# A hybrid attention and mLSTM block: three loads at the start of the kernel given to other queues, and the first block of x loaded in two halves

## The chip, the cores and the metric

The kernel runs on one core of one Trainium2 chip. The metric is the device time of one execution in microseconds. Before the change it was timed three times: median 314.51 us, from 314.25 to 314.80 us. One more execution was recorded by the hardware profiler; all rows below come from that one.

## The reference

`x` has 512 tokens of 1024 features. The block is one layer:

```
h    = rms_norm(x, pre_norm_g)
proj = h @ w_in                      # 1024 x (9*512 + 8) columns
aq, ak, av, az, mq, mk, mv, mo, mz, mi, mf = split_columns(proj)
ya = moba_attention(rope(aq), rope(ak), av)          # 8 heads of 64
ya = rms_norm(ya, attn_out_g) * silu(az)
hm = mlstm_chunkwise(silu(conv(mq)), silu(conv(mk)), mv, mi, mf)   # 4 heads of 128
ym = sigmoid(mo) * normalised(hm) * mlstm_out_g * silu(mz)
y  = concat(ya, ym) @ w_out
out = x + rms_norm(y, post_norm_g)
```

All in fp32. For this change only the start matters: `x` is scaled column by column with `pre_norm_g` and multiplied with the first 512 columns of `w_in` that are wanted, those of `mv`. The rms factor of each token is applied to the products afterwards.

## The kernel before, in words

Every fp32 operand of a product is split into a high part (fp32r) and a low part (the rest), and a product is three matmuls: high by high, low by high, high by low. The weights come in blocks of 128 x 512 (256 KB), called slots, numbered in the order of a table `SLOTS`. A slot lies first in one of 4 raw buffers (`w_raw`), its high part is made by ScalarE (`cut`, line 797) and its low part by VectorE (line 1072). Slot 0 is the exception: its high part is made by VectorE (line 1099).

`x` (`x_sb`, which the profile names by its arena, `farena`) is loaded in six column chunks: four of 128 columns (256 KB) and two of 256 columns (512 KB). A chunk of 128 columns is 512 rows of 512 bytes. TensorE turns each 128 x 128 block of x with `ident` into a PSUM bank (line 1542 for the first 128 columns, line 1549 for later ones). ScalarE writes the high part of the turned x, scaled with the gains of the norm (line 803 in two halves of 256 tokens for the first block, line 809 for later ones), and VectorE writes the low part (lines 1095 and 1088). The gains come as 8 rows of 128 in the tile `prow` (4 KB), which TensorE turns too (line 1537), and VectorE copies them from PSUM to `pcol` (line 1083).

All engines run their own list of instructions in order. What sets the order at the start:

- SyncE's queue (SP) issues, in this order, chunk 0 of x, weight slot 0, chunk 1 of x, slot 1, chunk 2, slot 2 and so on. From slot 4 on each issue waits until the low part of the slot four places earlier is made.
- ScalarE issues `prow` as its first instruction (line 826), then loads its activation table, and then waits for the first turned half of x.
- GpSimd clears `ident` (line 613), clears `prow2` (line 614), makes `ident` the identity (line 616), and then waits for the high part of slot 0 before its next work (lines 619 and on). Its own loads (lines 637 to 645: six small ones into `prow2`, one into `rope_sb`) come after that.
- VectorE waits for the turned gains, copies them, waits for slot 0, makes its high part (line 1099), then the two low halves of x, then the low part of slot 0.
- TensorE runs six matmuls on constants (`keep_busy`, line 1531), waits for `ident` and for `prow`, turns `prow` (line 1537), waits for all of chunk 0 of x, turns its four blocks of tokens (line 1542, two signals, one for each half of 256 tokens), runs two more constant matmuls of 256 columns, and then starts the products of slot 0 (line 1569).

The lines of TensorE's start:

```python
            keep_busy(6)
            pe.wait_ge(ident_done, 1)
            pe.wait_ge(par_in, 16)
            pe.transpose(bank[6][:, 0:R_AG], prow[:], ident[0:R_AG, 0:R_AG]).then_inc(par_ps, 1)
            ...
            turn_x_half(0)
            turn_x_half(1)
            keep_busy(2, AW // 2)
            for k in range(NK - 1):
                mv_slot(k)
```

In a product of slot 0 to 3 (`mv_slot`) the high by high matmuls of the four token tiles come first, then (for slot 0) the low by high ones, then the blocks of the next chunk of x are turned (`turn_x(k + 1)`), and the terms with the low part of the weights come last.

Of the kernel before, what the change touches and what calls it, by code (L numbers as in the profile page):

```python
# [23 lines left out]
P = 128  # L24
# [4 lines left out]
AW = 512  # L29
# [20 lines left out]
SLOTS = [("in", "cols", k, MVC) for k in range(NK - 1)]  # L50
# [16 lines left out]
X_CHUNKS = ((0, 1), (1, 1), (2, 1), (3, 1), (4, 2), (6, 2))  # L67
# [3 lines left out]
HALF_SEQ = SEQ // 2  # L71
# [10 lines left out]
def width(n):  # L82

    return MZ_W if S_MZ <= n < S_MZ + NK else AW
# [148 lines left out]
def unit(u):  # L233

    return NT - 1 - u // AH, u % AH
# [7 lines left out]
def build(nc, x, pre_g, w_in, i_bias, f_bias, conv_w, conv_b, attn_g, mlstm_g, w_out, post_g, rope, out):  # L243
    with ExitStack() as ctx:
        def sb(name, shape, dt=F32):
            return ctx.enter_context(nc.sbuf_tensor(name, shape, dt))

        def sem(name):
            return ctx.enter_context(nc.semaphore(name))
# [4 lines left out]
        w_raw = sb("w_raw", [P, RAW, AW])  # L254
# [14 lines left out]
        prow = sb("prow", [R_AG, P])  # L269
# [34 lines left out]
        def f_part(at, *shape):  # L304
            n = int(np.prod(shape))
            v = farena[:, at:at + n]
            return v if len(shape) == 1 else v.rearrange("p (a b) -> p a b", a=shape[0]) if len(shape) == 2 \
                else v.rearrange("p (a b c) -> p a b c", a=shape[0], b=shape[1])
# [7 lines left out]
        x_sb = f_part(F_X, NT, D)  # L316
# [65 lines left out]


        x_in = [sem(f"x_in{c}") for c in range(len(X_CHUNKS))]
        par_in = sem("par_in")
        rope_in = sem("rope_in")
        post_in = sem("post_in")
        raw_in = [sem(f"raw_in{r}") for r in range(RAW)]
# [124 lines left out]
        def low_done(eng, n):  # L513

            eng.wait_ge(w_lo_done[n % 2], n // 2 + 1)
# [4 lines left out]
        def turn_tile(n):  # L520

            _, kind, i = TURNS[n]
            return 0 if kind == "ym" else 4, NT - 1 - i


        def store(sp, i):
            t = NT - 1 - i
            for c in range(2):
                cols = slice(c * AW, (c + 1) * AW)
                sp.wait_ge(out_ready, 2 * i + c + 1)  # L530
                sp.dma_start(out[0, t * P:(t + 1) * P, cols], xr[i][:, cols]).then_inc(out_done[i], 16)

        @block.sync
        def _(sp):
            x2 = x.rearrange("b s d -> (b s) d")

            def load_x(c):
                k, n = X_CHUNKS[c]
                cols = slice(k * P, (k + n) * P)
                sp.dma_start(x_sb[:, :, cols], x2[:, cols].rearrange("(t p) d -> p t d", p=P)).then_inc(x_in[c], 16)  # L540

            def rows_out(w, m):

                sp.wait_ge(kq_ready, NT * w + m + 1)
                sp.dma_start(kq_dram[w, :, ROT * m:ROT * m + ROT, :], by_dims[:, m, :]).then_inc(kq_out[w], 16)

            def rows_back(w, m):

                sp.wait_ge(kq_out[w], 16 * NT)
                if w:  # L550
                    sp.wait_ge(kt_lo, NT)
                sp.dma_start(whole[:, m, :], kq_dram[w, 2 * m:2 * m + 2].rearrange("h d s -> (h d) s"))\
                    .then_inc(kq_moved[w], 16)

            for n, (mat, kind, k, c) in enumerate(SLOTS):
                if n in X_BEFORE:
                    load_x(X_BEFORE[n])
                if n >= RAW:
                    low_done(sp, n - RAW)
                w = w_in if mat == "in" else w_out  # L560
                if kind == "cols":
                    src = w[0, k * P:(k + 1) * P, c:c + width(n)]
                    dst = w_raw[:, n % RAW, 0:width(n)]
                else:
                    src = w[0, k * P:(k + 4) * P, c:c + MD].rearrange("(k p) c -> p k c", p=P)
                    dst = w_raw[:, n % RAW, :].rearrange("p (k c) -> p k c", k=4)
                sp.dma_start(dst, src).then_inc(raw_in[n % RAW], 16)
                if n == S_QK + 6:
                    sp.wait_ge(ssx_done, NT)
                    sp.dma_start(gains[:], attn_g.to_broadcast([P, AW])).then_inc(gain_in, 16)  # L570
                for w in range(2):
                    for c in range(2):
                        if n == OUT_AT[w] + c:
                            rows_out(w, 2 * c)
                            rows_out(w, 2 * c + 1)
                        if n == BACK_AT[w] + c:
                            rows_back(w, 2 * c)
                            rows_back(w, 2 * c + 1)
                if n == S_AQ + 4:
                    sp.wait_ge(az_gained, NT)  # L580
                    sp.dma_start(gains[:], mlstm_g.to_broadcast([P, AW])).then_inc(gain_in, 16)
            sp.wait_ge(v_lo_done, NT)
            sp.dma_start(post, post_g.to_broadcast([P, D])).then_inc(post_in, 16)

            def load_residual(i):
                t = NT - 1 - i
                sp.dma_start(xr[i], x2[t * P:(t + 1) * P, :]).then_inc(xr_in[i], 16)

            sp.wait_ge(ym_gated, NT)
            load_residual(0)  # L590
            load_residual(1)
            sp.wait_ge(turn_ps, TURN_OF["ym", NT - 1] + 1)
            load_residual(2)
            load_residual(3)
            store(sp, 0)
            store(sp, 1)
            store(sp, 2)
            sp.wait_ge(out_ready, 2 * NT - 1)
            sp.dma_start(out[0, 0:P, 0:AW], xr[NT - 1][:, 0:AW]).then_inc(out_done[NT - 1], 16)
            sp.wait_ge(out_ready, 2 * NT + 1)  # L600
            sp.dma_start(out[0, 0:P, quarter[1]], xr[NT - 1][:, quarter[1]]).then_inc(out_done[NT - 1], 16)
            for i in range(NT):
                sp.wait_ge(out_done[i], 32 + 16 * (i == NT - 1))
# [3 lines left out]
        def _(g):  # L607
# [2 lines left out]

            g.memset(ident[:], 0.0).then_inc(cleared, 1)
            g.memset(prow2[:], 0.0).then_inc(par2_clear, 1)
            g.wait_ge(cleared, 1)
# [170 lines left out]
        def _(a):  # L786
# [25 lines left out]
            def x_squares(t):  # L812
                if t:
                    a.wait_ge(ssx_done, t)
                for c in range(len(X_CHUNKS)):
                    a.wait_ge(x_in[c], 16)
                a.activation(silu_az[:, 0:2, :].rearrange("p a c -> p (a c)"), x_sb[:, t, :], ACT.Square, accum_out=ssx[:, t:t + 1]).then_inc(ssx_done, 1)

# [4 lines left out]
                a.activation(mv[:, t * MH:(t + 1) * MH, 0:MD], bank[t][:].rearrange("p (h d) -> p h d", h=MH), ACT.Copy,  # L823
                             scale=rx[:, t:t + 1]).then_inc(mv_hi_done, 1)

            a.dma_start(prow[:], pre_g.rearrange("o (c p) -> (o c) p", p=P)).then_inc(par_in, 16)
            a.activation(ssx[:, 0:1], ones, ACT.Copy)
            x_hi_half(0)
            x_hi_half(1)
# [1 line left out]
            for k in range(1, NK):  # L831
                cut(k)
                x_hi(k)
                if k >= 5:
                    x_squares(k - 5)
            cut(RING)
            x_squares(NT - 1)
            for n in range(RING + 1, RING + 6):
                cut(n)
# [160 lines left out]
            for s in range(STEPS):  # L1000
# [18 lines left out]
                for kind, what in events:  # L1019
# [7 lines left out]
                    elif kind == "y_sq":  # L1027
                        i, c = what
                        n = OUT_OF[i, c]
# [5 lines left out]
                    elif kind == "y_q_sq":  # L1035
                        q = what[0]
# [476 lines left out]
        def _(pe):  # L1513
# [23 lines left out]
            pe.transpose(bank[6][:, 0:R_AG], prow[:], ident[0:R_AG, 0:R_AG]).then_inc(par_ps, 1)  # L1537

            def turn_x_half(q):
                pe.wait_ge(x_in[0], 16)  # L1540
                for t in (2 * q, 2 * q + 1):
                    mm = pe.transpose(bank[4 + q][:, t * P:(t + 1) * P], x_sb[:, t, 0:P], ident[:])  # L1542
                mm.then_inc(xt_ps, 1)
# [129 lines left out]
# [6 lines that stand above are left out]
# [42 lines left out]
            for b in range(S_QK, LAST_SLOT):  # L1721
                if b < S_MZ and (b - S_QK) % 12 < 4:
                    n = 2 * ((b - S_QK) // 12) + (b - S_QK) % 12 // 2
# [35 lines left out]
            def turn(n):  # L1759

                _, kind, i = TURNS[n]
                t = NT - 1 - i
                pe.wait_ge(ym_gated if kind == "ym" else ya_gated, i + 1)
                pe.wait_ge(masked, min(TURNS[n][0], NU))
                src = ym[:, t] if kind == "ym" else silu_az[:, t]
                for k in range(4):
                    mm = pe.transpose(bank[TURN_BANK][:, k * P:(k + 1) * P], src[:, k * P:(k + 1) * P], ident[:])  # L1767
                mm.then_inc(turn_ps, 1)
# [85 lines left out]
            for s in range(STEPS):  # L1854
# [10 lines left out]
                if 0 <= u < NU:  # L1865
                    t, h = unit(u)
# [56 lines left out]
```

## Time and profile before

| | |
|---|---|
| median of three executions | 314.51 us (314.25 to 314.80) |
| profiled execution, its time | 314.27 us |
| profiled execution, its span | 312.5 us |
| TensorE busy | 306.0 us, 98% of the span |
| VectorE, ScalarE, GpSimd busy | 73%, 53%, 29% |
| mean granted clock of TensorE | 0.995 |
| read from HBM, written | 33.68 MB, 4.28 MB |

The span is the time from the first to the last recorded instruction; the execution's own time is 1.77 us more. Times in the rows are microseconds from the start of the span. PE is TensorE's matmul side, PEld its loading of weights, DVE VectorE, ACT ScalarE, POOL GpSimd, SP SyncE; a q behind a name is the engine's sequencer, which issues DMAs.

### The profile page before, as it was taken

The page shows a single profiled execution, that of the slowest core. Times are in us where ns is not written, and L with a number is a line of the kernel's source. Part 1 is how long each engine was busy: PE and PEld are TensorE (multiplying, and loading weights), DVE is VectorE, ACT ScalarE, POOL GpSimd, SP SyncE. Part 2 cuts the span into 40 slices and gives each one's busy share as a digit, 9 for nine tenths or more (in the row PEclk, how much of TensorE's full clock was granted, in tenths as well). Part 3 has the DMA queues.
Part 4 walks back from the last instruction along what each step waited for, and adds up shares of the span by engine and source line. Part 5 has one row for each costly group of instructions (what it writes and reads, how often), then busy time and mean ns, then how long its engine had stood idle before and what let it go on. Part 6 is the DMA issues. An engine that isn't in the chain of part 4 may idle for free.

```text
span 312.5 us, 5011 instructions
## 1 busy us (share of the span) xinstructions
PE 306.0 (98%) x1607; PEld 257.4 (82%) x1607; DVE 226.8 (73%) x510; ACT 165.2 (53%) x339; POOL 91.1 (29%) x110
## 2 busy tenths in 40 slices
PE   8999999999999999999999999999999999999992
PEld 5788888888888888888888899977888888888892
DVE  2644899956999499967999457996666867856534
ACT  3467694578337324384244583574746867353301
POOL 4501005164340004000040017569612983000000
PEclk9999999999999999999999999999999999999997
DMA  7933473565423546752555432410210473310111
GB/s 208 338 77 96 105 203 100 159 196 143 151 67 97 157 144 183 215 168 72 156 184 155 130 103 67 135 69 1 81 55 2 139 222 125 141 51 0 69 68 67
DMA packets 28953, 38.28 MB, mean 123 GB/s; under 512 B 2552, under 2 KB 16236, under 8 KB 28928
## 3 DMA queue, kind: packets, MB, share of 16 engines
q1 hardware_dynamic: 27440, 34.51, 37.2%
q0 software_dynamic: 1328, 3.32, 3.0%
q8 instruction: 13, 0.21, 0.3%
q10 hardware_dynamic: 160, 0.14, 0.1%
q14 instruction: 12, 0.10, 0.1%
HBM read 33.68 MB, written 4.28 MB: 121 GB/s over the span
## 4 chain that ended last, share of the span: by engine, by line
PE 94%; issue 3%; DVE 0%; DVEq 0%; ACT 0%; POOLq 0%; POOL 0%; ACTq 0%
PE bank L1516 25%; PE bank L1518 24%; PE bank L1517 24%; PE bank L1569 4%; PE bank L1873 3%; PE bank L1817 3%; PE bank L1838 3%; PE bank L1664 2%; PE bank L1767 1%; PE bank L1531 1%; PE bank L1549 1%; PE bank L1828 1%; PE bank L1665 1%; PE bank L1850 0%; PE bank L1542 0%
## 5 line engine op out<-in xcount | busy, mean ns | idle before, releaser
L797 ACT ACTIVATE w_hi<-w_raw 128x512 fp32r<-128x512 f32 (+1 forms) x73 | 44.4, 615 | 62.9 <-PE bank L1518 50.1
L1516 PE MATMUL bank<-w_hi,xT_hi 128*128 128x512 f32 (+2 forms) x180 | 71.1, 395 | 0.0
L1518 PE MATMUL bank<-w_hi,xT_lo 128*128 128x512 f32 (+2 forms) x180 | 68.1, 379 | 0.0
L1517 PE MATMUL bank<-w_lo,xT_hi 128*128 128x512 f32 (+2 forms) x180 | 67.8, 376 | 0.0
L1516 PE MATMUL bank<-xT_hi,w_hi 128*128 128x512 f32 x136 | 54.1, 397 | 0.0
L1072 DVE TENSOR_TENSOR w_lo<-w_raw,w_hi 128x512 fp32r<-128x512 f32 (+1 forms) x66 | 46.5, 715 | 9.7 <-ACT w_hi L797 9.5
L1518 PE MATMUL bank<-xT_hi,w_lo 128*128 128x512 f32 x136 | 53.3, 392 | 0.0
L1517 PE MATMUL bank<-xT_lo,w_hi 128*128 128x512 f32 x136 | 53.1, 391 | 0.0
L1518 PEld LDWEIGHTS bank<-w_hi,xT_lo 128*128 128x128 f32 x180 | 33.8, 188 | 5.8
L1516 PEld LDWEIGHTS bank<-w_hi,xT_hi 128*128 128x128 f32 x180 | 34.0, 189 | 5.0 <-POOL w_lo L685 0.4
L1517 PEld LDWEIGHTS bank<-w_lo,xT_hi 128*128 128x128 f32 x180 | 34.0, 189 | 4.5
L1518 PEld LDWEIGHTS bank<-xT_hi,w_lo 128*128 128x128 f32 x136 | 25.6, 188 | 5.6
L1517 PEld LDWEIGHTS bank<-xT_lo,w_hi 128*128 128x128 f32 x136 | 25.6, 188 | 4.7
L1516 PEld LDWEIGHTS bank<-xT_hi,w_hi 128*128 128x128 f32 x136 | 25.6, 188 | 4.6
L998 ACT ACTIVATE rarena<-bank 128x512 fp32r<-128x512 f32 (+3 forms) x32 | 14.0, 436 | 21.2 <-PE bank L1873 21.2
L1385 DVE CUSTOM_DVE_ANT_0 farena<-bank,causal 128x512 f32<-128x512 f32 (+3 forms) x32 | 15.4, 483 | 9.3 <-PE bank L1817 9.3
L1391 DVE TENSOR_TENSOR rarena<-bank,rarena 128x512 fp32r<-128x512 f32 (+3 forms) x32 | 15.6, 487 | 7.9 <-ACT rarena L998 7.8
L1180 DVE SCALAR_TENSOR_TENSOR farena<-farena,pcol 128x512 f32<-128x512 f32 x24 | 18.8, 782 | 0.9
L1200 DVE SCALAR_TENSOR_TENSOR farena<-bank,farena 128x512 f32<-128x512 f32 (+3 forms) x16 | 7.8, 490 | 15.8 <-PE bank L1518 15.5
L990 ACT ACTIVATE farena<-farena,mx 128x512 f32<-128x512 f32 (+3 forms) x32 | 17.9, 558 | 2.1 <-DVE mx L1385 2.0
L647 POOL TENSOR_TENSOR vr<-vs,mhalf 128x2 f32<-128x2 f32 x8 | 5.7, 709 | 43.3 <-DVE vs L1239 43.3
L1873 PE MATMUL bank<-ident,farena 128*128 128x128 f32 x80 | 14.7, 282 | 0.0
(213 smaller groups left out, 568.8 us busy)
## 6 DMA issues: line engine op xcount, KB each, us to landing
w_raw<-in_w_in SPq DMA_DIRECT2D x66, 256.0 KB, 2.9
w_raw<-in_w_out SPq DMA_DIRECT2D x16, 256.0 KB, 2.6
farena<-g_rows POOLq DMA_DIRECT2D x4, 640.0 KB, 4.2
kq_rows<-stage SPq DMA_DIRECT2D x8, 256.0 KB
gy<-kq_rows SPq DMA_DIRECT2D x8, 256.0 KB, 3.3
gy<-in_x SPq DMA_DIRECT2D x4, 512.0 KB, 5.0
out_y<-gy SPq DMA_DIRECT2D x7, 256.0 KB, 2.1
w_raw<-in_w_in SPq DMA_DIRECT2D x8, 196.0 KB, 3.3
```

The costliest lines, as they stand in the source:

```text
L797: a.activation(hi, raw, ACT.Copy).then_inc(w_hi_done, 1)
L990: a.activation(prob[:, s % 2, 0:n], sm[:, s % 2, 0:n], ACT.Exp, scale=-1.0, bias=mx[:, s:s + 1], accum_out=rsum[:, s:s + 1]).then_inc(prob ...
L998: a.activation(pT[:, 2 * (u % 2), 0:n], bank[4 + u % 2][:, 0:n], ACT.Copy).then_inc(pt_hi, 1)
L1072: v.tensor_tensor(lo, raw, hi, ALU.subtract).then_inc(w_lo_done[n % 2], 1)
L1180: ins = v.scalar_tensor_tensor(out=acc, in0=u[:, j:j + SEQ], scalar=tap[j], in1=acc, op0=ALU.mult, op1=ALU.add)
L1385: v.tensor_tensor_reduce(sm[:, s % 2, 0:n], bank[6 + s % 2][:, at:at + n], causal[:, SEQ - n:], -Q_SCALE, BIG, ALU.add, ALU.min, mx[:, s:s ...
L1391: v.tensor_tensor(pT[:, 2 * (u % 2) + 1, 0:n], bank[4 + u % 2][:, 0:n], f32(pT[:, 2 * (u % 2), 0:n]), ALU.subtract).then_inc(pt_lo, 1)
L1516: pe.matmul(o, hi, m_hi, start=start, stop=False)
L1517: pe.matmul(o, hi, m_lo, start=False, stop=False)
L1518: return pe.matmul(o, lo, m_hi, start=False, stop=stop)
L1569: mm = pe.matmul(bank[t][:], xs[:, k, t * P:(t + 1) * P], ws, start=k + term == 0, stop=False)
L1873: mm = pe.transpose(bank[4 + u % 2][:, j * P:(j + 1) * P], prob[:, u % 2, j * P:(j + 1) * P], ident[:])
```

## The change

Three loads change their queue and one is cut in two:

- `prow` (4 KB) is issued by GpSimd as its first instruction, ahead of the clearing of `ident`, and no longer by ScalarE.
- Weight slot 0 (256 KB) is issued by ScalarE as its first instruction, in the place of `prow`, and no longer by SyncE between chunks 0 and 1 of x.
- Chunk 0 of x is issued by SyncE as two DMAs of 128 KB, tokens 0 to 255 and tokens 256 to 511, each with a semaphore of its own. TensorE waits for the first before it turns tokens 0 to 255, and for the second before it turns tokens 256 to 511. The sum of squares on ScalarE (`x_squares`) waits for both.

```diff
+        x_half_in = [sem(f"x_half_in{q}") for q in range(2)]
...
             def load_x(c):
                 k, n = X_CHUNKS[c]
                 cols = slice(k * P, (k + n) * P)
+                if c == 0:
+                    for q in range(2):
+                        part = x2[q * HALF_SEQ:(q + 1) * HALF_SEQ, cols].rearrange("(t p) d -> p t d", p=P)
+                        sp.dma_start(x_sb[:, 2 * q:2 * q + 2, cols], part).then_inc(x_half_in[q], 16)
+                    return
                 sp.dma_start(x_sb[:, :, cols], x2[:, cols].rearrange("(t p) d -> p t d", p=P)).then_inc(x_in[c], 16)
...
             for n, (mat, kind, k, c) in enumerate(SLOTS):
                 if n in X_BEFORE:
                     load_x(X_BEFORE[n])
+                if n == 0:
+                    continue
...
+            g.dma_start(prow[:], rows_of(pre_g)).then_inc(par_in, 16)
             g.memset(ident[:], 0.0).then_inc(cleared, 1)
...
             def x_squares(t):
-                for c in range(len(X_CHUNKS)):
+                for q in range(2):
+                    a.wait_ge(x_half_in[q], 16)
+                for c in range(1, len(X_CHUNKS)):
                     a.wait_ge(x_in[c], 16)
...
-            a.dma_start(prow[:], pre_g.rearrange("o (c p) -> (o c) p", p=P)).then_inc(par_in, 16)
+            first_cols = SLOTS[0][3]
+            a.dma_start(w_raw[:, 0, :], w_in[0, 0:P, first_cols:first_cols + AW]).then_inc(raw_in[0], 16)
...
             def turn_x_half(q):
-                pe.wait_ge(x_in[0], 16)
+                pe.wait_ge(x_half_in[q], 16)
```

## Rows read from the trace of the kernel before

**Rows 1.** Busy time by stretch: us, then each engine's busy time, clock, DMA share, GB/s.

```profile
0.00:4.00 4.00, 3.15 (x8) 1.18 (x9) 0.17 (x1) 1.49 (x2) 0.84 (x7) 1.00 0.50 143
4.00:300.00 296.00, 296.00 (x1555) 249.98 (x1555) 223.10 (x500) 162.10 (x331) 89.75 (x102) 1.00 0.41 124
```

**Rows 2.** The chain that ended last, its first pieces: start, us, what.

```profile
0.84 2.72 PE bank L1531 x6
...
4.87 0.43 PE bank L1531 x2
5.29 2.04 PE bank L1569 x8
```

**Rows 3.** Timeline of the first 5 us: start, us, instruction, idle before it and releaser.

```profile
0.80 0.20 POOL L613 MEMSET ident<- 128x128 f32 x1 [0.29 <-POOLq L1915]
0.81 0.45 SPq L540 DMA_DIRECT2D farena<-in_x  x1
0.81 0.60 ACTq L826 DMA_DIRECT2D prow<-in_pre_norm_g  x1
...
1.25 0.29 POOL L616 TENSOR_SCALAR_AFFINE_SELECT ident<-ident 128x128 f32<-128x128 f32 x1
1.31 0.49 SPq L567 DMA_DIRECT2D w_raw<-in_w_in  x1
...
2.77 0.50 SPq L567 DMA_DIRECT2D w_raw<-in_w_in  x1
...
3.49 0.18 PEld L1537 LDWEIGHTS bank<-ident,prow 8*128 8x128 f32 x1 [0.83 <-issue]
...
3.75 0.72 PEld L1542 LDWEIGHTS bank<-ident,farena 128*128 128x128 f32 x4
...
4.48 0.90 ACT L803 ACTIVATE xT_hi<-bank,pcol 128x256 fp32r<-128x256 f32 x2 [1.53 <-PE bank L1542]
4.59 0.43 DVE L1099 CAST w_hi<-w_raw 128x512 fp32r<-128x512 f32 x1 [0.63 <-DMA w_raw<-in_w_in]
4.66 0.64 PE L1531 MATMUL bank<-const-bfloat16-1.0 128*128 128x256 bf16 x2
...
5.07 0.90 PEld L1569 LDWEIGHTS bank<-w_hi,xT_hi 128*128 128x128 f32 x4 [0.26 <-DVE w_hi L1099]
```

**Rows 4.** DMA issues in 0 to 1.2, 1.25 to 1.8 and 2.75 to 3.2: KB, us to landing.

```profile
farena<-in_x SPq DMA_DIRECT2D x1, 256.0 KB, 2.9
w_raw<-in_w_in SPq DMA_DIRECT2D x1, 256.0 KB, 3.2
w_raw<-in_w_in SPq DMA_DIRECT2D x1, 256.0 KB, 4.4
```

**Rows 5.** ScalarE's queue from 2.55 to 2.7 us: packets, MB, share of the DMA engines.

```profile
q10 hardware_dynamic: 1, 0.00, 0.4%
```

**Rows 6.** Small loads and stores issued by GpSimd, from 7.8, 52.8 and 64.9 us on.

```profile
prow<-in_attn_out_g POOLq DMA_DIRECT2D x1, 2.0 KB, 5.4
prow<-in_conv_b POOLq DMA_DIRECT2D x1, 4.0 KB, 4.9
g_rows<-gy POOLq DMA_DIRECT2D x1, 2.0 KB, 1.6
rope_rows<-farena POOLq DMA_DIRECT2D x1, 16.0 KB, 2.7
```

**Rows 7.** Busy time in two early stretches and one late, columns as in rows 1.

```profile
1.60:2.40 0.80, 0.80 (x3) 0.30 (x2) 0.00 (x0) 0.80 (x1) 0.00 (x0) 1.00 0.40 101
2.40:3.20 0.80, 0.80 (x3) 0.15 (x1) 0.00 (x0) 0.54 (x2) 0.00 (x0) 1.00 1.12 312
8.80:9.60 0.80, 0.80 (x4) 0.62 (x4) 0.73 (x2) 0.52 (x1) 0.80 (x3) 1.00 1.05 376
```

**Rows 8.** Timeline of slot 1's first use, around 7.2 to 8.6 us.

```profile
7.23 0.63 ACT L797 ACTIVATE w_hi<-w_raw 128x512 fp32r<-128x512 f32 x1 [1.85 <-DMA w_raw<-in_w_in]
...
8.61 0.76 PEld L1569 LDWEIGHTS bank<-w_hi,xT_hi 128*128 128x128 f32 x4 [0.35 <-issue]
```

## The prediction

> **What bounds the kernel now.** I read the busy time by stretch first. From 4 to 300 us TensorE is busy 296.00 of 296.00 us [rows 1]. So whatever moves TensorE's start of products moves the end by as much, and nothing later gives it back; and whatever leaves that start alone is worth nothing. Before 300 us only the first 4 have idle time on TensorE, 0.85 us, of which 0.84 lie before its first instruction [rows 1, 2]. Second, the chain that ended last: it is TensorE from 0.84 us on. Six constant matmuls (2.72 us), the turn of the gains, four turns of x, two constant matmuls (0.43 us), then products from about 5.1 us [rows 2]. The reader is to see that the loads do not stand in this chain. Third, since the chain shows only the last to come, the timeline, for how closely the loads miss it [rows 3], and the DMA issues for their landing [rows 4].
>
> Each load is needed and there as follows. `prow`: needed at 3.49, when the constant matmuls are through [rows 3]; the last packet of ScalarE's queue comes between 2.55 and 2.7 [rows 5], so it is about 0.8 us early. Chunk 0 of x: issued at 0.81, 2.9 us to landing, so 3.71 [rows 3, 4]; TensorE takes it up at 3.75, when the load of the gains' turn had ended at 3.49 + 0.18 = 3.67. At most 0.08 us of waiting. Slot 0: issued at 1.31, 3.2 us to landing, so 4.51 [rows 3, 4]; VectorE casts it from 4.59 to 5.02, TensorE loads from 5.07 after 0.26 us in which its load side waited for that cast [rows 3]. But the matmul side was not free before about 5.08: the two constant matmuls start at 4.66 and take 0.64 us to the end of the last, which streams its 256 columns in 0.21 (0.43 for two, rows 2), so the next could start at 4.66 + 2 x 0.21 = 5.08 [rows 2, 3]. The cast is late by hardly anything.
>
> **The change, part by part.**
>
> *Slot 0 on ScalarE's queue.* It is issued 0.50 us earlier (0.81 for 1.31). If it takes its 3.2 us it lands at 4.0; if it shares the DMA engines with the two halves of x and gets none of the gain, at 4.5. In the first case VectorE, done with the gains at 3.96 (4.59 less 0.63 idle, rows 3), casts from about 4.05 to 4.48, and the 0.26 us of the load side go. What is late next: the matmul side (5.08, above), and the high part of the first half of x, two activations of 0.90 us from 4.48 on, so 0.45 for one and 4.93 for the first [rows 3]. Gain from this part: from 5.10 to 5.08, 0.02 us; at the highest 0.1, if the first load may go in ahead at 4.95 and shortens the step from the constant matmuls to the products. ScalarE's own list is as before: one issue at 0.81 for another (0.60 for `prow`, 0.49 for a slot from SyncE), then the table load; its next work is at 4.48 after 1.53 us of idleness.
>
> *Two halves of x.* The first half has half the packets, and the DMA share of 1.12 from 2.4 to 3.2 us says that packets set the pace there [rows 7]. 256 KB at 312 GB/s are 0.84 us, so the first half could be there up to 0.42 us sooner, at 3.3, if it had the engines alone; sharing with slot 0 may eat all of it. Sooner than 3.67 it is worth nothing: the gain is at most the 0.08 us above. The second half is needed for the third turn, at 3.75 + 2 x 0.18 = 4.1 (0.72 for the four loads, rows 3). Bound above: x and slot 0 are 512 KB, 1.68 us at 312 GB/s, from about 1.95 (0.40 of a share in 1.6 to 2.4) to 3.6, and 0.4 for the landing as the worst, 4.0: still hidden. I take 0.05 gained. The extra issue on SyncE (0.45) stands where slot 0's (0.49) stood, so chunk 1 and slot 1 keep their issue times (2.77 for slot 1).
>
> *`prow` on GpSimd's queue.* GpSimd issues it at 0.80. Its issue may take what ScalarE's takes, 0.60 us; even with 1 us `ident`, done at 1.25 + 0.29 = 1.54 [rows 3], is done by 2.6, against 3.49. The cover is 0.9 us. The landing is what counts, and the trace has no GpSimd DMA on empty queues at the start. Its nearest rows go far apart: 1.6 us for 2 KB and 2.7 us for 16 KB in quiet stretches, 4.9 to 5.4 us for 2 and 4 KB while the loads run at a share of 1.05 [rows 6, 7]. From 0.80 that is 2.4 to 3.5 in the one case and 5.7 to 6.2 in the other. The limit is 3.49, 2.7 us after the issue. At the time of issue nothing moves: from 1.6 to 2.4 the engines are at 0.40, and full only after [rows 7]. That is nearer to the quiet rows, and I take 2.3 us, a landing at 3.1: hidden. Behind TensorE's wait stand all of its turns and products, and VectorE's copy and ScalarE's two activations (both need the gains), so every 0.1 us beyond 3.49 is 0.1 us of the end, or more.
>
> Here the Trainium skill speaks against the change. DMA: Bandwidth & Descriptors, in "Latency and other measured facts", gives about 1 us to the first byte for GpSimd's path against 0.6 for the hardware path, and for HBM 0.2 us on average but 2 us under high load. By the first figure an estimate of the landing is 0.4 us later than before, 3.0, and the sum is unchanged; with 2 us more it would be near 5 and the kernel some 1.5 us slower. The quiet and the loaded rows differ by about as much, so the trace agrees that load matters, and not which case the start is.
>
> *What follows.* Slot 1 lands at 2.77 + 4.4 = 7.2; ScalarE cuts it from 7.23 to 7.86, makes the next high part of x behind that, and TensorE starts slot 1 at 8.61 after 0.35 us without a load [rows 4, 8]. With slot 0 on another queue the ramp from 1.6 to 2.4 fills better, and slot 1 may be there up to 0.3 us earlier, (0.8 x 0.6 = 0.48 us of idle share, some of it usable). The matmuls themselves run through there, with about 0.1 us lost, so I count 0.03. The waits added in `x_squares` (one each in four calls) and the earlier start of GpSimd's clears (they wait for slot 0's cast, 0.5 us sooner) lie on engines with room: 0.
>
> **Sum.** 0.02 + 0.05 + 0.03 = 0.1 us gained. The profiled execution would go from 314.27 to 314.17; it was 0.24 below the median, so the median goes from 314.51 to 314.4. Bounds of the terms: gains of 0.1 + 0.08 + 0.1 = 0.3; losses of 0 to 2.7.
>
> One thing may halve even this. The constant matmuls of 512 columns take 0.45 us each, 2.72 for six, and eight product matmuls of 512 columns take 2.04, 0.26 each, while the granted clock reads 1.00 in both stretches [rows 1, 2]. That is the lower level of 1.2 GHz at first and 2.4 GHz later, and the rise falls at the first products. If it comes when it comes, products begun sooner run at the lower level.
>
> **The rivals.**
>
> *The gains come late (slower).* The place is TensorE's wait for `prow` at 3.49. For it: five microseconds in all loads of GpSimd that came amid the x and weight loads [rows 6]; in the changed kernel two queues start at once beside it. Against it: those stood behind a load that had been full for microseconds [rows 7]. Price: 5.7 to 6.2 less 3.49 is 2.2 to 2.7 us, 316.6 to 317.1. It decides from a landing 3.4 us after the issue on (4.2 us: 0.63 us late and 0.1 gained elsewhere). More can come on top: with TensorE idle there the clock may stay at the lower level, at 0.45 - 0.26 = 0.2 us for each 512-column matmul. Chance 0.15; a landing between 3.5 and 4.2, which gives 314.5 to 315.1, another 0.13.
>
> *The loads were late in other executions (faster).* The chain misses slot 0 and x by less than 0.1 us. Where a load lands later than in the profiled execution, the kernel before pays in full and the changed one, with 0.5 us of lead, does not. A spread there is likely: 256 KB took 2.9 to 4.4 us [rows 4]. But the profiled execution is only 0.24 below the median, so this is worth at most 0.24 more, 314.2; with all terms at their bounds 313.97. Beyond 0.63 us needs something that I do not see. Chance of a gain over 0.63: 0.08.
>
> *The queues only take turns.* ScalarE's and SyncE's queue feed the same DMA engines, at a share of 1.12 already [rows 7]: slot 0 gains what x loses, first half at 3.7 to 3.8, second at 4.0. Then nothing changes, or 0.1 us is lost: 314.5 to 314.6. Chance 0.2, inside the range of no change. The Trainium skill says so of the queues in DMA: Bandwidth & Descriptors, "Issuing engines are not separate DMA queues": only the issue time is saved. By that rule the 0.50 us of issue order are the whole of what slot 0 can win, and the forecast moves by 0.1 at most.
>
> **How the numbers follow.** A measurement of this kernel can tell about 0.2%, 0.63 us, from no change. Forecast as worked out (314.2 to 314.5): 0.44. Taking turns 0.2, slightly late gains 0.13: with the forecast 0.77 for no change. Faster 0.08, slower 0.15. The range reaches down to 313.9, with all bounds of the gains, and up to 315.6, which takes in gains that land up to 1.1 us late; what it leaves out is most of the late rival and the far faster case, under 0.2. The likeliest case alone: 314.1 to 314.8.
>
> **What the profile after would show.** `prow`: the gains' load (line 1537 before) still starts at 3.4 to 3.5; at a later time the wait is the gains'. Slot 0: VectorE's cast starts at 4.0 to 4.1, not 4.59. x: TensorE's first turn at 3.70, first product at 5.0 to 5.1. Slot 1: its cut at 6.9 to 7.3. The forecast is wrong if TensorE has a hole after the six constant matmuls, or if more product matmuls than one take 0.4 us.

## The result and the profile after

The changed kernel has a median of 316.95 us over 17 executions, the kernel before 314.53 us over 17 timed beside them. The ratio, which is one of means and not of medians, is 1.0059, with a 95% interval of 1.004 to 1.0078: slower by 0.6%, 1.9 us. The forecast was 314.4, no change. The ratios below compare with the kernel before in the same way. One execution of the changed kernel, at a granted clock of 0.846, is left out of the ratio and of what follows.

The executions fall into two groups, and this matters as much as the median:

| | executions | up to 316 us | above 316 us |
|---|---|---|---|
| before | 17 | 14, at 314.25 to 314.80 | 3, at 316.62 to 316.93 |
| changed | 16 | 4, at 315.30 to 315.56 | 12, at 316.60 to 318.32 |

So there are two losses: each group is later than its counterpart, by about 1 us below 316 and 0.5 us above, and most executions went from the first group to the second.

The profiled execution of the changed kernel took 315.30 us (span 313.6) and is of the lower group. Its busy time by stretch, columns as in [rows 1]:

```profile
0.00:4.00 4.00, 2.72 (x6) 0.72 (x6) 0.00 (x0) 1.49 (x2) 1.61 (x8) 1.00 0.46 122
4.00:300.00 296.00, 294.66 (x1547) 248.56 (x1548) 222.44 (x500) 162.37 (x331) 90.16 (x102) 1.00 0.42 124
10.00:300.00 290.00, 290.00 (x1524) 244.98 (x1523) 218.90 (x494) 159.77 (x327) 86.27 (x91) 1.00 0.41 120
```

TensorE ran 2.72 us of the first 4 where it was 3.15, and after 4 it stands idle for 1.34 us more. (A stretch in which TensorE stands idle is called a hole from here on.) From 10 us on it is busy without a break, as before. The loss is made in the first microseconds and nothing gives it back. The chain that ended last, its first pieces:

```profile
0.70 0.63 issue
1.33 3.65 DMA prow<-in_pre_norm_g
5.72 0.48 ACT xT_hi L812
6.34 2.06 PE bank L1581 x8
```

A load stands in the chain now, and it is the one of the gains on GpSimd's queue. The timeline, against [rows 3]:

```profile
0.81 0.95 SPq L544 DMA_DIRECT2D farena<-in_x  x2
0.81 0.44 ACTq L838 DMA_DIRECT2D w_raw<-in_w_in  x1
...
1.33 0.74 POOL L621 DMA_DIRECT2D prow<-in_pre_norm_g  x1 [0.82 <-POOLq L1927]
...
2.54 0.29 POOL L625 TENSOR_SCALAR_AFFINE_SELECT ident<-ident 128x128 f32<-128x128 f32 x1
...
5.12 0.20 PE L1549 MATMUL bank<-ident,prow 8*128 8x8 f32 x1 [1.56 <-DMA prow<-in_pre_norm_g]
...
5.25 0.66 PE L1554 MATMUL bank<-ident,farena 128*128 128x128 f32 x4
...
6.34 1.15 PE L1581 MATMUL bank<-w_hi,xT_hi 128*128 128x512 f32 x4 [0.22 <-ACT xT_hi L812]
```

GpSimd's load begins at 1.33, not at 0.80 where its clear of `ident` was, takes 3.65 us to landing, and TensorE stands still for 1.56 us: the hole behind the six constant matmuls that the prediction named as the sign that it is wrong. The products start at 6.34, where it was 5.10. `ident`, at 2.83, is in time. The landings of the other loads, as in [rows 4]:

```profile
w_raw<-in_w_in ACTq DMA_DIRECT2D x1, 256.0 KB, 3.5
farena<-in_x SPq DMA_DIRECT2D x1, 128.0 KB, 3.7
farena<-in_x SPq DMA_DIRECT2D x1, 128.0 KB, 3.5
```

Slot 0 lands at 0.81 + 3.5 = 4.3, 0.2 us sooner than before. But the first half of x lands at 0.81 + 3.7 = 4.5, where all of it was there at 3.7, and the second at 1.31 + 3.5 = 4.8. Had the gains been on time, x would have held TensorE for about 0.8 us; this is an estimate, 4.5 less the 3.75 of the first turn before.

### The profile page after: what moved, and what is told of

Same layout as the page of the kernel before. It is cut to its first block, busy times and chain, and to the rows that moved or that the text cites. A ratio compares the mean times of both kernels' runs of the same rounds, so it can differ in the third digit from the quotient of the medians.

```text
span 313.6 us, 5015 instructions
## 1 busy us (share of the span) xinstructions
PE 305.3 (97%) x1607; PEld 256.5 (82%) x1607; DVE 227.0 (72%) x510; ACT 165.5 (53%) x339; POOL 92.3 (29%) x111
## 4 chain that ended last, share of the span: by engine, by line
PE 93%; issue 3%; DMA 1%; DVE 0%; ACT 0%; DVEq 0%; POOLq 0%; POOL 0%; ACTq 0%
PE bank L1528 25%; PE bank L1530 24%; PE bank L1529 24%; PE bank L1581 4%; PE bank L1885 3%; PE bank L1829 3%; PE bank L1850 3%; PE bank L1676 2%; DMA prow<-in_pre_norm_g 1%; PE bank L1779 1%; PE bank L1561 1%; PE bank L1840 1%; PE bank L1677 1%; PE bank L1862 0%; DVEq L244 0%
```

## The experiments

### The parts one by one

**The changed kernel with the gains back on ScalarE's queue**, ahead of slot 0.

```diff
-            g.dma_start(prow[:], rows_of(pre_g)).then_inc(par_in, 16)
...
+            a.dma_start(prow[:], pre_g.rearrange("o (c p) -> (o c) p", p=P)).then_inc(par_in, 16)
             first_cols = SLOTS[0][3]
             a.dma_start(w_raw[:, 0, :], w_in[0, 0:P, first_cols:first_cols + AW]).then_inc(raw_in[0], 16)
```

> The changed kernel, with the load of the gains back on ScalarE's queue, ahead of slot 0. Theory A (the GpSimd load alone is what costs): the gains are there by 2.7 us as before, TensorE turns them at 3.5, and the time is 314.2 to 314.5. Theory B (two queues of big loads from the start also delay x: in the trace of the changed kernel the first half of x lands at 4.5 and slot 0 at 4.3): the gains' turn is at 3.5, but the first turn of x waits until about 4.5, so 0.7 us or more over the kernel before, 315.1 or more, and a share of executions at 316.5 or more stays.

Measured: ratio 1.0039 (1.0017 to 1.0062), median 316.73 us, 8 of 12 executions above 316. TensorE in its trace:

```profile
3.50 0.23 PE L1549 MATMUL bank<-ident,prow 8*128 8x8 f32 x1
3.65 0.44 PE L1554 MATMUL bank<-ident,farena 128*128 128x128 f32 x2
5.71 0.44 PE L1554 MATMUL bank<-ident,farena 128*128 128x128 f32 x2 [1.61 <-DMA farena<-in_x]
```

The gains are on time, at 3.50. The first half of x is too, but the second comes 4.3 us after its issue at 1.31, and TensorE waits 1.61 us in the middle of its turns. Slot 0 is late as well (1.45 + 4.0 = 5.45). Theory A, that GpSimd's load alone costs, has fallen. Theory B had the right size, and not the right half.

**The kernel before with only the gains on GpSimd's queue.** The same line is taken from ScalarE's list and put at the head of GpSimd's.

> The kernel before, with only the load of the gains moved to GpSimd's queue as its first instruction. Theory A: all of the loss is here, the gains land at 4.5 to 5.0 us, 316 to 317 as the changed kernel. Theory B: also slower, since TensorE waits for the gains alone, but x and slot 0 land at 3.7 and 4.5 as before; 315.5 to 317.

Measured: ratio 1.006 (1.0038 to 1.0082), 11 of 12 executions above 316.

```profile
farena<-in_x SPq DMA_DIRECT2D x1, 256.0 KB, 2.7
prow<-in_pre_norm_g POOLq DMA_DIRECT2D x1, 4.0 KB, 3.6
```

This one line reproduces the whole loss. The gains land at 1.33 + 3.6 = 4.9, with x there since 0.81 + 2.7 = 3.5. TensorE's hole is 1.45 us.

**The kernel before with only the halves of x.**

```diff
+                if c == 0:
+                    for q in range(2):
+                        part = x2[q * HALF_SEQ:(q + 1) * HALF_SEQ, cols].rearrange("(t p) d -> p t d", p=P)
+                        sp.dma_start(x_sb[:, 2 * q:2 * q + 2, cols], part).then_inc(x_half_in[q], 16)
+                    return
```

> The kernel before, with only chunk 0 of x cut into two halves on SyncE's queue. Both theories: x and slot 0 land within 0.5 us of before, 314.3 to 314.9. If slot 0, now third in the queue, lands 0.5 us later (its issue is 0.45 us later), theory B gives 314.8 to 315.1.

Measured: ratio 1.002 (0.9993 to 1.0046), so not told from no change; 5 of 12 above 316. In its trace both halves are early (2.3 and 2.4 us after their issues at 0.81 and 1.31), but slot 0, now third in the queue, is issued at 1.81 and takes 4.5 us; the cast waits, and the products start at 6.9. This profiled execution, at 317.26, is one of the five above 316 and not a usual one:

```profile
6.90 2.08 PE L1577 MATMUL bank<-w_hi,xT_hi 128*128 128x512 f32 x4 [1.66 <-DVE w_hi L1107]
```

**The kernel before with only slot 0 on ScalarE's queue**, behind the gains.

```diff
             a.dma_start(prow[:], pre_g.rearrange("o (c p) -> (o c) p", p=P)).then_inc(par_in, 16)
+            first_cols = SLOTS[0][3]
+            a.dma_start(w_raw[:, 0, :], w_in[0, 0:P, first_cols:first_cols + AW]).then_inc(raw_in[0], 16)
...
+                if n == 0:
+                    continue
```

> The kernel before, with only slot 0 moved to ScalarE's queue, behind the gains. Theory A: no loss, 314.2 to 314.6. Theory B: x, in one piece, shares with slot 0 and lands at 4.3 to 4.8 instead of 3.7: 315 to 315.5, with a share of executions at 316.5 or more.

Measured: ratio 1.005 (1.0022 to 1.0079), 6 of 11 above 316. It is slot 0 that is late, 1.45 + 4.0 = 5.45, and not x (3.0 us to landing), which theory B had at 4.3 or later. This one trace does not show that the second queue delays slot 0: with the first loads of the kernel before, it landed between 4.5 and 5.7 us (see below). That this arrangement is slower is shown by the eleven executions; how it loses is not. The first products in this trace:

```profile
6.03 2.08 PE L1573 MATMUL bank<-w_hi,xT_hi 128*128 128x512 f32 x4 [0.63 <-DVE w_hi L1103]
```

None of the three parts gains alone, and their losses (0.6, 0.2 and 0.5%) add up to more than the 0.6% of all together. That fits a TensorE that waits for the last of three loads and not for each in turn, though the 0.2% is not clear of noise.

### The second group: a hole and the clock

In three of the four traces above (gains on GpSimd, halves, slot 0) the first four products of 512 columns took 2.04 to 2.08 us, 0.5 each; in the profiled execution of the change they took 1.15, 0.29 each. These are TensorE's two levels, 1.2 and 2.4 GHz. The fourth trace, the changed kernel with the gains on ScalarE's queue, is another case: it was at the upper level before its hole (two turns of x in 0.44 us, above) and at the lower one after it, and there the granted clock says so, with 0.50 from 7 to 10 us and this from 8 to 12:

```profile
8.00:12.00 4.00, 4.00 (x16) 3.14 (x15) 1.75 (x3) 1.21 (x2) 4.00 (x10) 0.70 1.09 353
```

The next kernels are about that.

**The changed kernel once more**, to have a second trace.

> The changed kernel once more, for a second trace. Theory C: if it is of the group above 316.6, the gains land at about 5 as in the first trace and product matmuls take 0.4 us each for a while. Theory D: the gains or x land 1 us later or more and the matmuls take 0.23 us as in the first trace.

It took 317.93 us, span 316.2. **The changed kernel with ten constant matmuls instead of six**, which last to where the loads have landed:

```diff
-            keep_busy(6)
+            keep_busy(10)
```

> The changed kernel with ten constant matmuls ahead of the gains' turn instead of six, which at 0.45 us each last to about 5.3 us, past the landing of the gains. Theory C (a hole on TensorE before the first products leaves its clock at 1.2 GHz for longer in most executions, and that makes the group of executions at 316.6 to 318.3): the group vanishes or shrinks to a few, nearly all executions at 315.3 to 315.8. Theory D (that group comes from loads that land later still): the spread stays as it is, 316.6 to 318.3 in most executions.

Measured: all 11 executions at 315.45 to 316.20, median 315.71, ratio 1.0026 (1.0009 to 1.0044). The changed kernel had 1.0059 and 316.95 us: more work in front makes it faster, by 0.3% or 1.2 us in the median. The two intervals just touch and come from two chips; the groups are plainer, with 12 of 16 executions at 316.60 or more without the longer cover and none above 316.20 with it. The two traces side by side, first the changed kernel's second, then the one with ten:

```profile
5.34 0.24 PE L1549 MATMUL bank<-ident,prow 8*128 8x8 f32 x1 [1.77 <-DMA prow<-in_pre_norm_g]
5.51 1.11 PE L1554 MATMUL bank<-ident,farena 128*128 128x128 f32 x4
...
6.85 2.04 PE L1581 MATMUL bank<-w_hi,xT_hi 128*128 128x512 f32 x4
```

```profile
2.08 3.19 PE L1543 MATMUL bank<-const-bfloat16-1.0 128*128 128x512 bf16 x7
...
6.81 1.16 PE L1581 MATMUL bank<-w_hi,xT_hi 128*128 128x512 f32 x4
```

The products start within 0.04 us of each other (6.85 and 6.81), and the gains land within 0.1 (1.33 + 3.9, 1.33 + 3.8). Only the four first product matmuls take 2.04 us in the one and 1.16 in the other. TensorE's busy time from 8 to 12 us, first the changed kernel, then the one with ten:

```profile
8.00:12.00 4.00, 4.00 (x14) 3.23 (x13) 1.19 (x2) 0.51 (x1) 4.00 (x11) 1.00 1.09 353
```

```profile
8.00:12.00 4.00, 4.00 (x22) 3.10 (x22) 2.50 (x4) 1.38 (x3) 4.00 (x11) 1.00 1.08 355
```

Busy for all 4 us in both, with 14 matmuls in the one and 22 in the other. That is TensorE at 1.2 and at 2.4 GHz, while both rows read a granted clock of 1.00. The spans differ by 1.8 us (316.2 and 314.4). The eight matmuls more, at 0.22 us each, are that difference. So this execution of the second group lost 1.8 us to the clock, beside one whose products start at the same time.

**The kernel before with two constant matmuls instead of six.** `keep_busy(2)`; no load is touched.

> The kernel before with two constant matmuls instead of six: no load is moved, TensorE only idles from about 1.8 to 3.5 us. Theory C: 1 to 2.5 us slower in most executions (315.5 to 317), with product matmuls at 0.4 us each after 5.1 us. Theory D: 314.3 to 314.6, since every load lands as before and the turns start at the same 3.5.

Measured: ratio 1.0043 (1.0022 to 1.0064), all 12 executions at 315.49 or above, 8 above 316. Less work in front costs 1.3 us. In its trace slot 0 landed late too (4.4 us, at 5.7), so that single execution has two causes. The loads are those of the kernel before, which has most of its executions below 315, so late loads do not explain all twelve: theory C, the clock, fits, and theory D alone does not. No trace of a usual one of these twelve was taken, nor of the unchanged kernel before above 316; for its group the late clock is inferred from these runs.

This trace shows one thing more. TensorE is ready for the gains at 1.85 us here, and has them, from ScalarE's queue, at 2.37:

```profile
2.37 0.24 PE L1537 MATMUL bank<-ident,prow 8*128 8x8 f32 x1 [0.52 <-DMA prow<-in_pre_norm_g]
```

That is 1.55 us after the issue at 0.82, with x on its way beside it. GpSimd's queue took 3.6 to 3.9 us from 1.33 for the same 4 KB. How much of this is the queue and how much the later start, no run separates.

### How long GpSimd's load takes, and why it starts late

**The changed kernel with all other loads behind the gains.** A wait for `par_in` stands ahead of the first issue on SyncE and on ScalarE.

> The changed kernel, but SyncE and ScalarE issue nothing until the gains have landed. It tells how long GpSimd's small load takes on idle DMA engines. Theory E (its 3.7 us from issue to landing are contention): 1.6 to 2.0 us, as the small GpSimd loads of the quiet stretches. Theory F (the first GpSimd load has a fixed cost): 3 us or more. The kernel is slower in either case, by 2 to 4 us, as x and slot 0 start later.

```profile
prow<-in_pre_norm_g POOLq DMA_DIRECT2D x1, 4.0 KB, 1.9
```

On idle engines the same load takes 1.9 us, beside the loads of x and slot 0 it takes 3.6 to 3.9 (four traces). Theory E, contention, has about half of it. It still starts at 1.33, so it lands at 3.2, in time for the 3.50 of the gains' turn by 0.3 us only. The kernel is 1.2% slower (median 318.53 us), as the other loads come after it.

**The changed kernel with GpSimd's load behind the making of `ident`.**

> The changed kernel with GpSimd's load of the gains behind the making of the identity instead of ahead of the clearing of it. In the trace of the changed kernel it starts at 1.33, 0.5 us after the other queues' first. If that is a fixed start of GpSimd's first load, it starts 0.5 us after the identity, at 2.0 or later, and the gains land later still, at 5.5 or so. If it is hidden by other work, it starts at about 1.55 and lands as in the changed kernel.

```profile
1.76 0.74 POOL L626 DMA_DIRECT2D prow<-in_pre_norm_g  x1 [0.22 <-issue]
...
6.21 0.20 PE L1549 MATMUL bank<-ident,prow 8*128 8x8 f32 x1 [2.64 <-DMA prow<-in_pre_norm_g]
...
7.43 2.04 PE L1581 MATMUL bank<-w_hi,xT_hi 128*128 128x512 f32 x4 [0.22 <-ACT xT_hi L812]
```

The identity is done at 1.53, the load starts at 1.76. The half microsecond before GpSimd's first load is thus mostly hidden when it has other work first; neither forecast was right, the truth lies between. The load takes 4.3 us from 1.76 and the hole grows to 2.64 us. After it the four turns of x take 0.66 us, so the level is still or already the upper one; then it falls, and as in the trace with the gains on ScalarE's queue the granted clock shows the fall, 0.67 from 8 to 12 us:

```profile
8.00:12.00 4.00, 4.00 (x16) 3.17 (x14) 1.86 (x3) 0.69 (x2) 4.00 (x10) 0.67 1.08 354
```

### Covering the loads of the kernel before

**The kernel before with ten constant matmuls instead of six.**

> The kernel before with ten constant matmuls instead of six at the start, as the changed kernel had in the run before (there all executions lay between 315.45 and 316.2). TensorE turns the gains at 5.3, when every load of the start has landed. If the late start of the loads and the clock are all there is, this is the same as that run, 315.5 to 315.9 with no execution above 316.3, so that the three moved loads cost nothing once they are covered. If the moved loads also disturb later ones, it is below that run by 0.3 us or more.

Measured: all 12 executions at 314.75 to 315.76, median 315.23, ratio 0.9997 (0.9977 to 1.0018). None is above 316, where 9 of 23 of the kernel before were on the same chip. Against the changed kernel with ten (1.0026, 1.0009 to 1.0044) it is lower by 0.3%; the intervals overlap, and they come from two chips. In its trace the clock rose early, so that ten constant matmuls ended at 4.84 and not at 5.27. In such an execution the changed kernel's gains, at about 5.1, would still be missing; whether that is the difference was not shown. The forecast for the case that the moved loads cost nothing once covered, 315.5 to 315.9, was missed on the low side.

**The kernel before with four, and with eight, constant matmuls of 256 columns ahead of the first product**, where slot 0 is waited for.

```diff
-            keep_busy(2, AW // 2)
+            keep_busy(4, AW // 2)
```

> The kernel before with four constant matmuls of 256 columns between the turns of x and the first product instead of two. They cost 0.2 us each at 1.2 GHz, up to 0.43 together, where slot 0 is on time, and keep TensorE busy until 5.5 where it is late. Theory C: the usual execution is 0.1 to 0.4 us slower, and the group above 316 (about one in five of the kernel before) gets smaller. Theory D: the group stays at one in five.

> The kernel before with eight constant matmuls of 256 columns between the turns of x and the first product instead of two. They keep TensorE busy from 4.6 to between 5.3 (at 2.4 GHz, 0.11 us each) and 6.3 (at 1.2 GHz, 0.21 each), past the landing of slot 0 in every trace so far. Theory C: no execution or at most one in twelve above 316, all others between 314.4 and 315.5, as with ten constant matmuls at the very start, but earlier by some tenths. Theory D: one in four above 316, as the kernel before on the same chip.

Measured: with four 314.05 to 315.18 and one execution at 317.01, ratio 0.9986 (0.9963 to 1.0009); with eight 314.31 to 315.59, none above 316, ratio 0.9982 (0.9959 to 1.0005). In the trace with four, slot 0 landed at 1.32 + 4.0 = 5.3, 0.8 us later than in the first trace of the kernel before, and yet the products ran at once at the upper level:

```profile
5.45 0.43 DVE L1099 CAST w_hi<-w_raw 128x512 fp32r<-128x512 f32 x1 [1.48 <-DMA w_raw<-in_w_in]
...
5.93 1.20 PE L1569 MATMUL bank<-w_hi,xT_hi 128*128 128x512 f32 x4 [0.81 <-DVE w_hi L1099]
```

Its time was 314.96. But the level had come up at about 4.5 us, before any of the four constant matmuls, which took 0.61 us together, so this trace does not show what the two added ones do. Over the three kernels with a longer cover 1 of 36 executions is above 316; of the kernel before, 16 of the 40 timed beside them (for the one with four alone it is 1 of 12 against 9 of 23, too few to tell). The group goes, and this is clear; the median hardly moves, and neither ratio is clear of 1. No version here beats the kernel before for certain.

## Why the prediction was wrong

**What bounds the kernel** held: TensorE without a break, so that its start moves the end. First product +1.24 us (5.10 to 6.34), span +1.1.

**The landing of the gains is the step that failed.** The prediction put it at 3.1 us, "nearer to the quiet rows", because the DMA engines are idle at the time of issue. It was 5.0. Two things were wrong in it. GpSimd's load started at 1.33 and not at 0.80: the start was read from a clear, which is no DMA. And the state of the engines at the issue was not what counted: the load takes 1.9 us when nothing else is issued until it lands, and 3.6 to 3.9 beside x and the weights, which start in the same microsecond. Of the two ends kept, 1.6 to 2.7 and 4.9 to 5.4 us, the truth lies between, and "It decides from a landing 3.4 us after the issue on" would have been met by 3.65 alone. The rival had this mechanism at a chance of 0.15, and its 316.6 to 317.1 us hold the median of 316.95, but by luck: it took the landing for 0.7 to 1.2 us later than it was and left the clock out of the price, and the two errors partly cancel. The figures quoted from DMA: Bandwidth & Descriptors of the Trainium skill, under "Latency and other measured facts", did point there: with the high HBM load that page names, the estimate was near 5, where the gains did land. The trace agrees with that size; which of the page's causes it was, no run here shows.

**The clock was named and not priced.** The prediction said that the clock may stay low if TensorE idles, at 0.2 us a matmul, as something on top. It is 1.8 us (the two traces whose products start at 6.85 and 6.81), more than the 1.24 us of the late start itself, and it is what moves the median: 12 of 16 executions above 316 instead of 3 of 17. Ten constant matmuls take this part away.

**The halves of x and slot 0** were counted as 0.05 and 0.02 us gained, at most 0.1 each. Slot 0 did land sooner (4.3), inside the bounds given (4.0 to 4.5). The first half of x landed at 4.5, where 3.3 to 3.8 was allowed; and the second at 4.8, where 4.0 was called the worst. Working out landings from bytes at 312 GB/s failed: the stretch from 1.6 to 2.4 moved 69 GB/s where 101 were moved before, and the next 189 where 312 were. The 0.4 us for the landing in that worst case came from no row. With the gains on time on ScalarE's queue, the other moves still cost 0.39%, 1.2 us. The rival of the queues taking turns saw that slot 0 gains what x loses, and priced it at 0 to 0.1 us. Taken alone, slot 0 on ScalarE's queue costs 0.5%.

**Slot 1** was taken to keep its issue at 2.77. It was issued at 2.32 and cut at 6.70, where 6.9 to 7.3 was forecast. The 2.77 belonged to the one trace, in which the issue of chunk 1 took 0.88 us; in five traces of kernels that leave SyncE's list alone it took 0.43, and slot 1 was issued at 2.32 or 2.33. What that gained cannot be told from the rest; 0.03 us had been counted for it.

**The profiled execution was taken for the usual one.** From its 0.24 us below the median the prediction concluded that late loads were worth at most 0.24 us. But the kernel before has a group of its own above 316: 31 of the 114 executions timed in all. Slot 0 landed at 4.5 us in that one trace, and at 4.6, 4.9, 5.3 and 5.7 in four others with the same loads (the kernel before with ten constant matmuls, with eight and with four at the products, and with two). The three times that were at hand all came from the lower group.

What stays open: what sets the landing of slot 0 in one execution, which with the same bytes came at 4.3 to 6.3 us over the arrangements and at 4.5 to 5.7 in one and the same; and what decides whether the clock is up after a hole. Its length does not: it was up after 1.56 and 2.64 us, and not after 1.45 and 1.77.

## What to carry to other kernels

When TensorE's first products wait for loads, do not ask only when the load lands, ask what happens if it lands a microsecond late: a hole before the first products costs its own length and, in most executions here, up to 1.8 us more for the clock. A few more constant matmuls made the usual execution 0.05, 0.3 and 0.6 us slower (four, eight, ten; means of the executions below 316), and brought 35 of 36 executions to between 314.05 and 315.76 us. Here the load on which everything waits was worst off on GpSimd's queue, and big loads on a second queue did not pay: with slot 0 issued at the same moment, the first 128 KB of x took 3.7 to 3.9 us to landing (four traces), with slot 0 issued 0.6 or 1.0 us later 2.2 and 2.3 (two). The difference is more than the 0.84 us that slot 0's bytes take at 312 GB/s. And a single trace of a kernel whose loads are just in time shows one draw of several.

## What the runs showed of the hardware

- GpSimd's first load starts 0.5 us after those of SyncE and ScalarE (1.33 for 0.81), in all five traces in which it is GpSimd's first work; with 0.7 us of other work ahead of it, 0.22 us of that start are still visible.
- A load of 4 KB on GpSimd's queue takes 1.9 us on idle DMA engines and 3.6 to 4.3 us beside the first loads of x and of the weights (five traces). On ScalarE's queue the same load, issued at 0.82, was there 1.55 us later.
- TensorE ran 14 or 22 matmuls in 4 busy us with a granted clock of 1.00 in both records. Where the durations show the lower level from the start on, as in the first 3.4 us of every trace, the record reads 1.00; where they show the upper level first and a fall after it (holes of 1.61 and 2.64 us), the record falls to 0.50.
- Where TensorE was busy up to the rise to the upper level, the durations put it between 3.5 and 6.4 us (six traces, of which the kernel before has 5.2). Where the first products ran at the lower level and the record at 1.00, it came only after 9.5 us (six traces).
- Six constant matmuls up to 3.56 us, then a hole of 1.56 us, and the clock was up (four turns of x within 0.66 us); six, then holes of 1.45 and 1.77 us, and it was not (1.11 us for the same four).
